# Expert weights: pair 3 of the first expert stage, and quarters 2 and 3 of odd pairs, in pieces of 2 MB

## The chip, the cores and the metric

The kernel runs on one core of a Trainium2 chip. The metric is the device time of one execution in microseconds (us), as the median of repeated runs. The inputs and weights lie in the chip's memory (HBM), all in 32-bit floats, and the kernel has to read them itself.

## The reference, cut to what matters

The program is a small network of four layers over 256 tokens of width 1024. Two layers mix retention and block attention. A third layer (RWKV-like mixing) and a fourth (differential attention and a state space model, "s5") are each followed by a mixture of experts. The change touches only the two mixtures of experts:

```
def hier_moe(h, w_group, b_group, w_expert, b_expert, w_gate, w_up, w_down):
    ...
    top_p, top_j = lax.top_k(e_prob, MOE_TOP_K)
    gates = g_w[:, None] * top_p / jnp.sum(top_p, axis=-1, keepdims=True)
    ...
    y = routed_experts(hf, expert_idx, gates, w_gate, w_up, w_down)

    def run_block(args):
        tok, e, gt = args
        xb = h_pad[tok]
        hidden = jax.nn.silu(xb @ w_gate[e]) * (xb @ w_up[e])
        return (hidden @ w_down[e]) * gt[:, None].astype(xb.dtype)
```

There are 32 experts in each stage, with w_gate and w_up of 1024x512 and w_down of 512x1024. Each token goes to two of them, so nearly every expert has work and the kernel reads all of them: 32 x 3 x 512 x 1024 x 4 bytes = 201 MB a stage.

## The kernel before, in words

An expert stage (`expert_functions`) works on 16 **pairs** of experts, numbered 0 to 15. The weights of a pair are 12 MB, laid out as six **pieces** of 2 MB (128 partitions x 16 KB). Pieces 0 to 3 are the **quarters** of gate and up (a quarter is 256 of the 1024 input features), and pieces 4 and 5 are the **halves** of down. In HBM two neighbouring pieces lie side by side, so pieces 0+1, 2+3 or 4+5 can be had with one transfer of 4 MB with rows of 32 KB (a "wide" load).

TensorE (PE) does for each pair, in this order (`of_pair`): quarters 0 to 3 (L3160, 16 profile records each, results in one PSUM bank), two transposes (L3190), the gathering of the next pair's tokens (L3127), the transposes of the hidden layer (L3197), down half 0 and half 1 (L3174), and the scattering back to the tokens (L3208). `gate_up` and `down` wait with `arrived` for the weights. For a piece that came in a wide load only its even piece has a wait, since both share one semaphore. The last pair of a stage has a form of its own, `of_last`: after each of quarters 0, 1 and 2 it issues six filler matmuls (`keep_clock`, L2814, 12 records), which compute nothing that is used. Further fillers stand later in it.

SyncE (SP) issues all weight loads from one queue, strictly in the order of the code (`sync`). In front of each load stands `released`, a wait until PE has used up what lies in the destination. With several pieces in one load, SP waits for the last of them. Bank 0 means even pairs, bank 1 odd pairs.

- Stage 0 (layer 3 of 4, semaphores moe0) has one set of six slots, the ring, from pair 3 on. Pair 0 is in the ring before the stage starts and pair 1 in spare memory elsewhere (`second`). Pair 2 goes to ring slots 1 to 5 and a spare slot (`third`). Half 1 of pair 1 takes part of ring slot 0. Then comes pair 3, which is written out by hand (L2954 to L2963): pieces 0+1 wide, three small transfers with s5 parameters (512 KB each), pieces 2+3 wide, piece 4, piece 5. Pairs 4 to 15 are loaded by `load_later` in a loop.
- Stage 1 (layer 4, moe1) has two sets of slots, so its loads run two pairs ahead. `load_later` serves it from pair 3 on.
- `alone` lists for each bank the pieces that `load_later` loads one by one. Before: none in even pairs, 4 and 5 in odd pairs.

After stage 0 the same queue sends the next layer's weights into the ring (L262).

Of the kernel before, what the change touches and what calls it, by code (L numbers as in the profile page):

```python
# [40 lines left out]
SLOTS = 6  # L41
# [2810 lines left out]
class Experts:  # L2852


    def __init__(self, g, ly, c0, router):
        self.sync, self.scalar, self.vector, self.tensor, self.gpsimd = expert_functions(g, ly, c0, router)


def expert_functions(g, ly, c0, router):
# [3 lines left out]
    nc, A, ps = g.nc, g.A, g.ps  # L2863
# [8 lines left out]
    landed = g.moe_landed[ly]  # L2872
    first = [[w] for w in ring]
    if ly == 0:
        second = [[g.spare], extra[0], extra[1], extra[2], extra[3], [g.xs_flat, ring[0][:, 0:2048]]]
        third = first[1:] + [[g.spare]]
        later = [first, first]
        later_wide = [moe_ring_wide(g, c0), moe_ring_wide(g, c0)]
        lag = 1
    else:  # L2880
# [3 lines left out]
        later = [first, second]  # L2884
        later_wide = [moe_ring_wide(g, c0), wide]
        lag = 2
    pieces = lambda where: [len(parts) for parts in where]
    early = [[a + b for a, b in zip(pieces(first), pieces(third))],
             pieces(second) if ly == 0 else [1, 1, 2, 1, 1, 2]]
    alone = ((), (4, 5))  # L2890

    def up_w(where, j, e):

# [17 lines left out]
    def turns(eng):  # L2911
        eng.wait_ge(router.s_turns, 1)
        return eng.value_load(g.turns[0:1, 0:1], min_val=1, max_val=S // CAP)
# [11 lines left out]
    def sync(sp):  # L2925
        def released(j, n, more):
            sp.wait_ge(*((s_gu, n * 4 + (more * 4 + j - 3)) if j < 4 else ((s_da, s_dn)[j - 4], n + more)))


        def load(where, bank, pair, j):  # L2930

            sp.dma_start(where[j][0], moe_piece(A, ly, pair, j)).then_inc(landed[bank][j], 16)

        def load_later(bank, pair, n, more):

            for d in range(SLOTS // 2):
                if 2 * d in alone[bank]:
                    for j in (2 * d, 2 * d + 1):
                        released(j, n, more)
                        load(later[bank], bank, pair, j)  # L2940
                else:
                    released(2 * d + 1, n, more)
                    sp.dma_start(later_wide[bank][d], A["moe_weights"][ly, pair, d]).then_inc(landed[bank][2 * d], 16)

        if ly == 0:
            released(0, 0, 1)
            router.part_of(sp, 5, 1, second[5][1])
            for j in range(SLOTS):
                if j < 5:
                    released(j + 1, 0, 1)  # L2950
                else:
                    released(0, 0, 2)
                load(third, 0, 2, j)
            released(5, 0, 2)  # L2954
            for d in range(2):
                released(2 * d, 0, 3)
                sp.dma_start(later_wide[1][d], A["moe_weights"][ly, 3, d]).then_inc(landed[1][2 * d], 16)
                if d == 0:
                    for dst, name in ((g.s5.B[:, 0], "s5_b"), (g.s5.C[0], "s5_c"), (g.s5.bT, "s5_bT")):
                        sp.dma_start(dst, A[name]).then_inc(g.s5_bc_landed, 16)  # L2960
            for j in alone[1]:
                released(j - 1, 0, 3)
                load(later[1], 1, 3, j)  # L2963
        else:
            for j in range(SLOTS):
                released(j, 0, 1)
                load(third, 0, 2, j)
            load_later(1, 3, 0, 2)
        T = turns(sp)
        with sp.Fori(0, T) as t:  # L2970
            with sp.Fori(0, NP // 2 - 2) as i:
                for bank in range(2):
                    load_later(bank, i * 2 + (4 + bank), t * NP + i * 2, 5 + bank - lag)
            with sp.If(t < T - 1):
                for pair in range(4):
                    load_later(pair % 2, pair, t * NP, NP + pair + 1 - lag)
        g.limit = len(g.chunks)
        g.free_when = {}
        if c0 < g.limit:
            for j in range(SLOTS):  # L2980
                sp.wait_ge(*((s_gu, T * NP * 4) if j < 4 else ((s_da, s_dn)[j - 4], T * NP)))
                g.send(sp, c0 + j + 1)
        else:
            for j in range(4):
                at = (slice(None), j // 2, slice((j % 2) * 512, (j % 2 + 1) * 512))
                sp.wait_ge(s_add, j + 1)
                sp.dma_start(g.out[0].rearrange("(a p) n -> p a n", p=P)[at], g.x[at]).then_inc(g.out_written, 16)
            sp.wait_ge(g.out_written, 64)
# [133 lines left out]
    def tensor(pe):  # L3122
# [19 lines left out]
        def arrived(bank, j, rounds):  # L3142

            if j % 2 == 0 or j in alone[bank]:
                pe.wait_ge(landed[bank][j], rounds * 16 + 16 * early[bank][j])

        def arrived_early(pair, j):

# [2 lines left out]
        def gate_up(quarter, where, bank, rounds):  # L3151
            if rounds is None:
                arrived_early(bank, quarter)
            else:
                arrived(bank, quarter, rounds)
            for k in range(2):
                for which in range(2):
                    for e in range(2):
                        q = (2 * which + e) * CAP
                        ins = pe.matmul(b_gu[q:q + CAP, :], xg[:, 2 * quarter + k, e * CAP:(e + 1) * CAP],  # L3160
                                        up_w(where, quarter, e)[:, which, k, :], start=(quarter == 0 and k == 0),
                                        stop=(quarter == 3 and k == 1), tile_position=(0, q))
            ins.then_inc(s_gu, 1)

        def down(half, where, bank, rounds):
            if rounds is None:
                arrived_early(bank, 4 + half)
            else:
                arrived(bank, 4 + half, rounds)
            for f in range(2):  # L3170
                for nh in range(2):
                    for e in range(2):
                        q = (2 * nh + e) * CAP
                        ins = pe.matmul(b_dn[q:q + CAP, :], hidT[:, 2 * half + f, e * CAP:(e + 1) * CAP],  # L3174
                                        down_w(where, 4 + half, e)[:, f, nh * 512:(nh + 1) * 512],
                                        start=(half == 0 and f == 0), stop=(half == 1 and f == 1), tile_position=(0, q))
            return ins
# [75 lines left out]
        if ly == 0:  # L3253
# [10 lines left out]
            router.keep_clock(pe, 5)  # L3264

    return sync, scalar, vector, tensor, gpsimd if ly == 0 else None


# [10 lines left out]
def moe_ring_wide(g, c0):  # L3279

    firsts = MOE_SLOTS[::2] if c0 == N_LOW else range(0, SLOTS, 2)
    return [g.ring[:, at:at + 2, :].rearrange("p s n -> p (s n)") for at in firsts]


def moe_piece(A, ly, pair, j):

    return A["moe_weights"][ly, pair, j // 2][:, (j % 2) * SW:(j % 2 + 1) * SW]
# [104 lines left out]
```

## Time and profile before

| | |
|---|---|
| median of 3 runs | 1549.54 us (1548.98 to 1549.82) |
| the profiled execution's own time | 1549.55 us |
| its span in the trace | 1547.4 us |
| PE busy | 1302.0 us (84%) |
| DVE, ACT, POOL busy | 458.6, 278.1, 265.8 us |
| read from HBM | 495.11 MB, 321 GB/s over the span |
| stage 0, about | 540 to 980 us of the span |
| stage 1, about | 1119 to 1543 us of the span |

The page cuts the span into 40 slices of 38.7 us. For each slice it gives the busy tenths of the engines, the clock that TensorE was granted (PEclk, 9 is 90% or more of full speed), and the busy share and rate of the 16 DMA engines. A busy DMA share of 9 at about 430 GB/s, slice after slice, marks the two expert stages. Between them lies the fourth layer's mixing part, where the DMA engines are partly idle. "Idle before" in a row of the timeline is the time in which the engine did nothing before that instruction, with the one that ended it.

### The profile page before, as it was taken

The page shows a single profiled execution, that of the slowest core. Times are in us where ns is not written, and L with a number is a line of the kernel's source. Part 1 is how long each engine was busy: PE and PEld are TensorE (multiplying, and loading weights), DVE is VectorE, ACT ScalarE, POOL GpSimd, SP SyncE. Part 2 cuts the span into 40 slices and gives each one's busy share as a digit, 9 for nine tenths or more (in the row PEclk, how much of TensorE's full clock was granted, in tenths as well). Part 3 has the DMA queues.
Part 4 walks back from the last instruction along what each step waited for, and adds up shares of the span by engine and source line. Part 5 has one row for each costly group of instructions (what it writes and reads, how often), then busy time and mean ns, then how long its engine had stood idle before and what let it go on. Part 6 is the DMA issues. An engine that isn't in the chain of part 4 may idle for free.

```text
span 1547.4 us, 22048 instructions
## 1 busy us (share of the span) xinstructions
PE 1302.0 (84%) x9344; PEld 711.9 (46%) x9344; DVE 458.6 (30%) x904; ACT 278.1 (18%) x545; POOL 265.8 (17%) x158
## 2 busy tenths in 40 slices
PE   9999999999999997766766767999999676677676
PEld 5754466547878543322322323656544232232233
DVE  2454663654945520200100100276411010010011
ACT  2142410433321210210000000215211011011010
POOL 0675236640000008591000000000000000000000
PEclk9999999999999999888888998999999888888889
DMA  9922562336431798999999999945799999999997
GB/s 372 364 114 82 200 228 71 154 142 274 162 125 42 289 393 357 438 425 431 434 434 426 435 427 431 377 157 208 287 423 429 427 437 429 429 434 430 430 437 296
DMA packets 34355, 498.19 MB, mean 322 GB/s; under 512 B 5488, under 2 KB 8304, under 8 KB 12016
## 3 DMA queue, kind: packets, MB, share of 16 engines
q1 hardware_dynamic: 34288, 497.22, 77.2%
q8 instruction: 52, 0.85, 0.2%
q14 instruction: 15, 0.12, 0.0%
HBM read 495.11 MB, written 2.10 MB: 321 GB/s over the span
## 4 chain that ended last, share of the span: by engine, by line
PE 43%; DMA 23%; another core or an unknown queue 5%; DVE 3%; ACT 1%; issue 1%; SPq 0%; DVEq 0%; ACTq 0%
DMA weight_ring<-in_moe_weights 19%; PE banks L3160 14%; PE banks L3174 5%; PE banks L3127 3%; PE banks L338 3%; DMA x_normed_hT_mix<-in_moe_weights 3%; PE banks L3208 2%; PE banks L1777 2%; PE banks L1970 2%; PE banks L2573 2%; PE banks L2482 1%; PE banks L2814 1%; PE banks L1318 1%; PE banks L1902 1%
## 5 line engine op out<-in xcount | busy, mean ns | idle before, releaser
L3160 PE MATMUL banks<-weight_ring,spare_weights_arena 128*32 128x512 f32 x1472 | 211.3, 724 | 143.1 <-DMA weight_ring<-in_moe_weights 141.5
L3070 DVE TENSOR_TENSOR spare_weights_arena<-spare_weights_arena,banks 64x512 f32<-64x512 f32 x32 | 22.1, 690 | 671.7 <-ACT spare_weights_arena L2993 671.7
L3160 PEld LDWEIGHTS banks<-weight_ring,spare_weights_arena 128*32 128x32 f32 x1472 | 56.0, 129 | 287.7 <-issue 268.5
L2993 ACT ACTIVATE spare_weights_arena<-banks 64x512 f32<-64x512 f32 x32 | 18.9, 592 | 509.8 <-PE banks L3160 509.8
L3127 PE MATMUL banks<-spare_weights_arena,x 128*128 128x64 f32 x960 | 110.5, 273 | 0.0
L3127 PEld LDWEIGHTS banks<-spare_weights_arena,x 128*128 128x128 f32 x960 | 109.6, 192 | 0.0
L3174 PE MATMUL banks<-weight_ring,spare_weights_arena 128*32 128x512 f32 x728 | 95.0, 661 | 12.0 <-issue 6.1
L986 POOL TENSOR_TENSOR weight_ring<-spare_weights_arena,weight_ring 128x2048 f32<-128x2048 f32 x16 | 74.0, 4632 | 70.4 <-DVE spare_weights_arena L830 38.5
L1099 PE MATMUL banks<-weight_ring,x_normed_hT_mix 128*128 128x512 f32 x192 | 84.8, 593 | 0.0
L3208 PE MATMUL banks<-spare_weights_arena 64*128 64x512 f32 x240 | 59.6, 615 | 21.0 <-ACT spare_weights_arena L2999 21.0
L3160 PE MATMUL banks<-x_normed_hT_mix,spare_weights_arena 128*32 128x512 f32 x272 | 42.2, 773 | 31.6 <-DMA x_normed_hT_mix<-in_moe_weights 31.6
L338 PE MATMUL banks<-weight_ring,x_normed_hT_mix 128*128 128x512 f32 x128 | 56.3, 595 | 0.0
L1067 PE MATMUL banks<-x_normed_hT_mix,weight_ring 128*128 128x256 f32 x256 | 56.0, 379 | 0.0
L3174 PEld LDWEIGHTS banks<-weight_ring,spare_weights_arena 128*32 128x32 f32 x728 | 26.9, 119 | 61.1 <-issue 51.2
L1099 PEld LDWEIGHTS banks<-weight_ring,x_normed_hT_mix 128*128 128x128 f32 x192 | 35.7, 190 | 41.5 <-issue 41.4
L986 POOL TENSOR_TENSOR weight_ring<-weight_ring 128x512 f32<-128x512 f32 (+1 forms) x14 | 37.9, 2724 | 81.6 <-DMA weight_ring<-in_ring_weights 74.5
L1067 PEld LDWEIGHTS banks<-x_normed_hT_mix,weight_ring 128*128 128x128 f32 x256 | 48.4, 190 | 7.6 <-issue 1.2
L3208 PEld LDWEIGHTS banks<-spare_weights_arena 64*128 64x128 f32 x240 | 20.7, 186 | 62.3 <-ACT spare_weights_arena L2999 48.2
L3051 DVE TENSOR_TENSOR spare_weights_arena<-banks,spare_weights_arena 128x256 f32<-128x256 f32 x64 | 27.0, 425 | 62.1 <-PE banks L3127 62.0
L3160 PE MATMUL banks<-spare_weights_arena 128*32 128x512 f32 x304 | 35.6, 607 | 11.7 <-DMA spare_weights_arena<-in_moe_weights 11.7
L2999 ACT COPY spare_weights_arena<-banks 128x512 f32<-128x512 f32 x32 | 18.8, 587 | 139.5 <-PE banks L3174 139.5
L1073 PE MATMUL banks<-weight_ring,x_normed_hT_mix 128*128 128x512 f32 x96 | 41.8, 593 | 0.2 <-DVE x_normed_hT_mix L415 0.2
(547 smaller groups left out, 1841.5 us busy)
## 6 DMA issues: line engine op xcount, KB each, us to landing
weight_ring<-in_moe_weights SPq DMA_DIRECT2D x50, 4096.0 KB, 25.2
weight_ring<-in_moe_weights SPq DMA_DIRECT2D x37, 2048.0 KB, 13.7
weight_ring<-in_ring_weights SPq DMA_DIRECT2D x35, 2048.0 KB, 12.1
spare_weights_arena<-in_moe_weights SPq DMA_DIRECT2D x21, 2048.0 KB, 49.6
spare_weights_arena<-in_moe_weights SPq DMA_DIRECT2D x7, 4096.0 KB, 54.5
x_normed_hT_mix<-in_moe_weights SPq DMA_DIRECT2D x7, 4096.0 KB, 51.8
weight_ring<-in_ring_weights SPq DMA_DIRECT2D x4, 1024.0 KB, 5.9
x_normed_hT_mix<-in_moe_weights SPq DMA_DIRECT2D x4, 1024.0 KB, 4.8
```

The costliest lines, as they stand in the source:

```text
L338: ins = pe.matmul(bank, lhsT[:, k, tt * P:(tt + 1) * P], w[:, k, n], start=(k == 0), stop=(k == k_all - 1))
L986: sub = lambda out, left, right: pool.tensor_tensor(out, left, right, ALU.subtract)
L1067: ins = pe.matmul(bank[:, hh * S:(hh + 1) * S], w[:, k, h * P:(h + 1) * P], g.hT[:, k, :], start=(k == 0), stop=(k == KT - 1))
L1073: ins = pe.matmul(bank, g.hT[:, k, half * P:(half + 1) * P], w[:, k, :], start=(k == 0), stop=(k == KT - 1))
L1099: ins = pe.matmul(at_ps[n - 1], left[:, k, :], right[:, k, :], start=(n != P2 and k == 0), stop=(k == HT - 1), skip_group_check=n in (P1, P2))
L1777: ins = pe.matmul(bank[:, i * S:(i + 1) * S], w[:, kt, n:n + P], g.hT[:, kt, :], start=(kt == 0), stop=(kt == KT - 1))
L1970: ins = pe.matmul(ps[j], g.mixT[:, kt, tt * P:(tt + 1) * P], w[:, kt, :], start=(kt == 4), stop=(kt == 3))
L2573: ins = pe.matmul(ps[j], g.mixT[:, k, tt * P:(tt + 1) * P], w[:, k, :], start=(k == 4), stop=(k == 3))
L3127: ins = pe.matmul((b_x, b_dn)[k // 4][:, k % 4 * 2 * CAP:(k % 4 + 1) * 2 * CAP], g.x[:, tt, k * P:(k + 1) * P], Pr[:, tt, :], start=(tt == ...
L3160: ins = pe.matmul(b_gu[q:q + CAP, :], xg[:, 2 * quarter + k, e * CAP:(e + 1) * CAP], up_w(where, quarter, e)[:, which, k, :], start=(quart ...
L3174: ins = pe.matmul(b_dn[q:q + CAP, :], hidT[:, 2 * half + f, e * CAP:(e + 1) * CAP], down_w(where, 4 + half, e)[:, f, nh * 512:(nh + 1) * 512],
L3208: pe.matmul(ps[2 * tt + nh][:, :], PT[r, tt * P:(tt + 1) * P], y[r, :], start=opens, stop=True, skip_group_check=True).then_inc(s_sum[2 * ...
```

## The change

In both stages pieces 2 and 3 of odd pairs are now loaded one by one (`alone`), as 4 and 5 already were. In stage 0, pair 3 is loaded in six single pieces, and each load has its own `released` wait. Piece 0 waits only for half 1 of pair 1, whose data lay in ring slot 0. Piece j after that waits for piece j-1 of pair 2, whose data lay in ring slot j. Before, the wide load 0+1 waited for both conditions of its two pieces, and so did 2+3 with theirs. On PE, quarter 3 of odd pairs gets a wait of its own. The count that the wait for quarters 0 and 1 compares with goes up by one load in stage 0, since pair 3 now brings those two quarters as two loads.

```
-    alone = ((), (4, 5))
+    pair_3_apart = 1 if ly == 0 else 0
+    alone = ((), (2, 3, 4, 5))
...
-            released(5, 0, 2)
-            for d in range(2):
-                released(2 * d, 0, 3)
-                sp.dma_start(later_wide[1][d], A["moe_weights"][ly, 3, d]).then_inc(landed[1][2 * d], 16)
-                if d == 0:
+            for j in range(SLOTS):
+                if j == 0:
+                    released(5, 0, 2)
+                else:
+                    released(j - 1, 0, 3)
+                if j == 1:
+                    sp.dma_start(later[1][1][0], moe_piece(A, ly, 3, 1)).then_inc(landed[1][0], 16)
+                else:
+                    load(later[1], 1, 3, j)
+                if j == 0:
                     for dst, name in ((g.s5.B[:, 0], "s5_b"), (g.s5.C[0], "s5_c"), (g.s5.bT, "s5_bT")):
                         sp.dma_start(dst, A[name]).then_inc(g.s5_bc_landed, 16)
-            for j in alone[1]:
-                released(j - 1, 0, 3)
-                load(later[1], 1, 3, j)
...
             if j % 2 == 0 or j in alone[bank]:
-                pe.wait_ge(landed[bank][j], rounds * 16 + 16 * early[bank][j])
+                pe.wait_ge(landed[bank][j], rounds * 16 + 16 * (early[bank][j] + (pair_3_apart if (bank, j) == (1, 0) else 0)))
```

SP's queue at pair 3 of stage 0. `first_e_normed` is the semaphore here that counts quarters done (`s_gu`), and `moe0_down` counts pairs whose half 1 is done. Before:

```order
L2932 DMA spare_weights_arena<-in_moe_weights 128x4096 [waits first_e_normed]
L2957 DMA weight_ring<-in_moe_weights 128x8192 [waits first_e_normed,moe0_down]
L2960 DMA spare_weights_arena<-in_s_b 128x1024
L2960 DMA spare_weights_arena<-in_s_c 128x1024
L2960 DMA spare_weights_arena<-in_s_bT 128x1024
L2957 DMA weight_ring<-in_moe_weights 128x8192 [waits first_e_normed]
L2932 DMA weight_ring<-in_moe_weights 128x4096 [waits first_e_normed]
L2932 DMA weight_ring<-in_moe_weights 128x4096 [waits moe0_down_half]
```

And now:

```order
L2933 DMA spare_weights_arena<-in_moe_weights 128x4096 [waits first_e_normed]
L2933 DMA weight_ring<-in_moe_weights 128x4096 [waits moe0_down]
L2966 DMA spare_weights_arena<-in_s_b 128x1024
L2966 DMA spare_weights_arena<-in_s_c 128x1024
L2966 DMA spare_weights_arena<-in_s_bT 128x1024
L2961 DMA weight_ring<-in_moe_weights 128x4096 [waits first_e_normed]
L2933 DMA weight_ring<-in_moe_weights 128x4096 [waits first_e_normed] x3
L2933 DMA weight_ring<-in_moe_weights 128x4096 [waits moe0_down_half]
```

The first load of pair 3 and the three s5 transfers behind it no longer wait for a quarter of pair 2. The wait for that quarter now stands in front of piece 1.

PE's queue in the last pair of stage 0, quarters 2 and 3 with the filler matmuls between them. Before:

```order
L3160 MATMUL banks<-weight_ring,spare_weights_arena 32x512 [waits moe0_odd_pairs_landed_2,first_e_root]
L3160 MATMUL banks<-weight_ring,spare_weights_arena 32x512 x7
L2814 MATMUL banks<-resident_constants 128x128 x6
L3160 MATMUL banks<-weight_ring,spare_weights_arena 32x512 x8
L3220 MATMUL banks<-resident_constants,spare_weights_arena 128x128 [waits first_mixT]
```

And now:

```order
L3163 MATMUL banks<-weight_ring,spare_weights_arena 32x512 [waits moe0_odd_pairs_landed_2]
L3163 MATMUL banks<-weight_ring,spare_weights_arena 32x512 x7
L2814 MATMUL banks<-resident_constants 128x128 x6
L3163 MATMUL banks<-weight_ring,spare_weights_arena 32x512 [waits moe0_odd_pairs_landed_3]
L3163 MATMUL banks<-weight_ring,spare_weights_arena 32x512 x7
L3223 MATMUL banks<-resident_constants,spare_weights_arena 128x128 [waits first_mixT]
```

Quarter 3 has a landing to wait for, and quarter 2 now waits for 2 MB where it waited for 4.

## Rows read from the trace of the kernel before

**Rows 1.** The page: section 2, slices of 38.7 us, and section 4, the chain by line.

```profile
DMA  9922562336431798999999999945799999999997
...
DMA weight_ring<-in_moe_weights 19%; PE banks L3160 14%; PE banks L3174 5%; PE banks L3127 3%; PE banks L338 3%; DMA x_normed_hT_mix<-in_moe_weights 3%; PE banks L3208 2%; PE banks L1777 2%; PE banks L1970 2%; PE banks L2573 2%; PE banks L2482 1%; PE banks L2814 1%; PE banks L1318 1%; PE banks L1902 1%
```

**Rows 2.** Windows: stretch, its length, busy us by engine, clock, DMA share, GB/s.

```profile
580.00:586.00 6.00, 5.30 (x41) 1.62 (x40) 0.00 (x0) 0.59 (x1) 3.85 (x14) 1.00 0.00 0
612.00:962.00 350.00, 245.07 (x1740) 106.86 (x1740) 35.16 (x85) 31.75 (x63) 67.36 (x66) 0.87 1.00 431
```

**Rows 3.** Timeline of SP's loads, 578 to 606 us: start, duration, line, operation.

```profile
585.10 0.34 SPq L2957 DMA_DIRECT2D weight_ring<-in_moe_weights  x1
...
590.18 7.19 SPq L2932 DMA_DIRECT2D weight_ring<-in_moe_weights  x2
```

**Rows 4.** Timeline of PE, 578 to 613 us; idle before in brackets.

```profile
579.84 0.59 PE L3174 MATMUL banks<-weight_ring,spare_weights_arena 128*32 128x512 f32 x1
...
583.05 7.07 PE L3160 MATMUL banks<-weight_ring,spare_weights_arena 128*32 128x512 f32 x64
...
601.32 3.64 PE L3160 MATMUL banks<-weight_ring,spare_weights_arena 128*32 128x512 f32 x32
612.28 5.56 PE L3160 MATMUL banks<-weight_ring,spare_weights_arena 128*32 128x512 f32 x32 [7.32 <-DMA weight_ring<-in_moe_weights]
```

**Rows 5.** The chain in order of time, stage 0: start, duration, what.

```profile
641.48 6.36 PE banks L3160 x32
...
670.62 5.44 PE banks L3160 x32
...
699.85 6.19 PE banks L3160 x32
```

**Rows 6.** Line 2932, all its loads: shortest, median, longest time to landing.

```profile
DMA to landing us min/median/max: 7.5/23.8/54.4
```

**Rows 7.** Line 2932, window 948.5 to 950: half 1 of stage 0's last pair.

```profile
L2932 SPq DMA_DIRECT2D weight_ring<-in_moe_weights x1: 332/332/332, 949.3 to 949.3; - x1
...
DMA to landing us min/median/max: 22.9/22.9/22.9
```

**Rows 8.** Line 2932, window 940 to 948.5: half 0 of the same pair.

```profile
L2932 SPq DMA_DIRECT2D weight_ring<-in_moe_weights x1: 333/333/333, 947.5 to 947.5; - x1
...
DMA to landing us min/median/max: 19.8/19.8/19.8
```

**Rows 9.** Timeline of PE, end of stage 0.

```profile
957.93 1.60 PE L2814 MATMUL banks<-resident_constants 128*128 128x128 f32 x12
962.49 1.92 PE L3160 MATMUL banks<-weight_ring,spare_weights_arena 128*32 128x512 f32 x16 [2.96 <-DMA weight_ring<-in_moe_weights]
...
965.88 1.92 PE L3160 MATMUL banks<-weight_ring,spare_weights_arena 128*32 128x512 f32 x16
...
972.45 4.68 PE L3174 MATMUL banks<-weight_ring,spare_weights_arena 128*32 128x512 f32 x32
```

**Rows 10.** Timeline of PE, end of stage 1.

```profile
1523.27 1.60 PE L2814 MATMUL banks<-resident_constants 128*128 128x128 f32 x12
1526.14 1.92 PE L3160 MATMUL banks<-x_normed_hT_mix,spare_weights_arena 128*32 128x512 f32 x16 [1.26 <-DMA x_normed_hT_mix<-in_moe_weights]
...
1529.53 1.92 PE L3160 MATMUL banks<-x_normed_hT_mix,spare_weights_arena 128*32 128x512 f32 x16
...
1535.52 3.64 PE L3174 MATMUL banks<-spare_weights_arena 128*32 128x512 f32 x32
```

**Rows 11.** Line 2932, window 1482 to 1484: half 1 of stage 1's last pair.

```profile
L2932 SPq DMA_DIRECT2D spare_weights_arena<-in_moe_weights x1: 333/333/333, 1482.7 to 1482.7; - x1
...
DMA to landing us min/median/max: 53.1/53.1/53.1
```

**Rows 12.** Timeline of PE after stage 0: the next layer's first projection.

```profile
984.62 3.83 PE L2482 MATMUL banks<-x_normed_hT_mix,weight_ring 128*128 128x128 f32 x32
```

**Rows 13.** Line 262, window 967 to 968: the load that this projection reads.

```profile
DMA to landing us min/median/max: 9.2/9.2/9.2
```

## The prediction, made before the result

> **What bounds the kernel now.** I read the page first. Its slices show the DMA engines at 9 tenths through both expert stages, and by line the largest share of the chain that ended last is a weight load, 19% plus 3% for the one into x_normed_hT_mix [rows 1]. The windows say how full that is: from 612 to 962 us the DMA share is 1.00 at 431 GB/s, while PE is busy 245 of 350 us [rows 2]. So within a stage only two things move its end: the time the DMA engines need for the bytes, and any time in which their queue is empty. What PE does in between counts only if it releases a slot too late, or after the last landings. Three places were left to look at: where the stage begins, what a piece costs, and what follows the last landings.
>
> The beginning has a hole. From 580 to 586 us the DMA share is 0.00 and 0 GB/s, with PE busy 5.30 of 6 us [rows 2]. SP's timeline says why: the next load, pieces 0+1 of pair 3, goes out at 585.10 [rows 3]. That is when PE has finished quarter 0 of pair 2, a quarter of the 7.07 us that began at 583.05. Its other condition, half 1 of pair 1, had ended at 579.84 + 0.59 = 580.43 [rows 4]. PE pays for the hole at 612.28, after 7.32 us of waiting for pieces 2+3 of pair 3 [rows 4]. From there the stage runs in step with the landings.
>
> At the end of each stage PE stands still until pieces 2+3 of the last pair are there (2.96 us in stage 0, 1.26 us in stage 1), and only then does quarter 2, then fillers, then quarter 3 [rows 9, 10].
>
> **The hole (gain 4.6 us).** Piece 0 of pair 3 now waits for 580.43 alone. SP issues 0.06 us after PE's last instruction of that kind (quarter 3 ends at 583.05 + 7.07 = 590.12, the load stands at 590.18 [rows 3, 4]), so at 580.5 instead of 585.1: 4.6 us. For this to count, the queue must not run empty again behind it. It then holds 2 MB and the three s5 transfers, 3.5 MB or 8.5 us at 431 GB/s, which lasts to about 589. Piece 1 goes out at 585.1, when quarter 0 of pair 2 is done, pieces 2, 3 and 4 by 590.18, when its last quarter is, and piece 5 at 597, the second of the two loads that began at 590.18 [rows 3]. Every one is in the queue before the one ahead of it is through. PE reaches pair 3 at 601.32 as before [rows 4], since it is busy with pair 2 until then. Its quarters 0 and 1 landed long before. Pieces 2+3 land at 612.28 - 4.6 = 607.7, later than PE's 601.32 + 3.64 = 605.0, so the whole 4.6 us reaches PE. At each later step the landings lead, and the shift stays. Bounds: no more than the hole itself, whose end is fixed by 585.10 - 580.43 = 4.7 us. If pair 3 were not limited by its landings it would be 0. I take 4.6, because PE's wait of 7.32 us exceeds it.
>
> **The price of a single piece (loss 1.1 us).** A 4 MB load becomes two of 2 MB in pair 3 of stage 0 twice, in its pairs 5, 7, ... 15 once (6), and in pairs 3, 5, ... 15 of stage 1 once (7), 15 in all. The trace has the same comparison already: the step from one landing of 2+3 to the next holds 4+5 once wide (even pairs) and once single (odd pairs). Wide: 670.62 - 641.48 = 29.14. Single: 699.85 - 670.62 = 29.23 [rows 5]. That is 0.09 us a split here; the nine further steps of the stage repeat the pattern between 29.14 and 29.23, and I take 0.07. 15 x 0.07 = 1.1 us (0.6 in stage 0, 0.5 in stage 1), all of it on the path, since the DMA engines are the path. Bounds: 0 at one end. At the other end stands a load into an empty queue, which took 7.5 us to land [rows 6], where inside a full queue two such landings lie 949.3 + 22.9 - (947.5 + 19.8) = 4.9 us apart [rows 7, 8]. That would be 2.6 us a split. The rows of the full queue are the same case as ours, so I stay at 0.07. The instructions added on SP (fourteen in its program, some 0.3 us per load) lie beside its waits.
>
> The Trainium skill, "DMA: Bandwidth & Descriptors", section on the anatomy of one DMA, fits a transfer as about 2.0 us fixed plus bytes / 436 GB/s. Read as a cost for each transfer in turn, it would speak against this change: 15 more transfers would be 30 us. The spacing of 4.9 us for 2 MB above is the bytes alone at 431 GB/s, so the trace agrees only with the second term while the queue is full. The fixed part shows up only when the queue was empty.
>
> **The end of stage 0 (gain 3.0 us).** Piece 2 of the last pair now lands one piece, 4.9 us, ahead of piece 3, at 962.4 - 4.9 = 957.5 on the old time scale. PE is then still in the fillers behind quarter 1, which begin at 957.93 and take 1.5 (as after quarter 2: from 962.49 + 1.9 to 965.88). So quarter 2 runs from 959.5 to 961.3, its fillers to 962.9, and quarter 3, landed at 962.4, begins at 962.9 instead of 965.88 [rows 9]. What follows hangs on quarter 3 only: silu, transposes, hidden layer, down at 972.45 - 3.0 = 969.5, where half 0 has landed (947.5 + 19.8 = 967.3 [rows 8]). Half 1 lands at 949.3 + 22.9 = 972.2 [rows 7] and takes 1.8 us of PE (3.64 / 2 at full clock [rows 10]), so down can't end before 974.0. Before, it ended at 977.1, and 3.0 less is 974.1. The two limits meet. The gain is 3.0, at most 3.1. PE's clock sets the lower bound: down took 4.68 us here, against 3.64 in the same work at full clock [rows 9, 10]. If the half level (1.2 GHz instead of 2.4) falls on both quarters and the fillers between, 1.6 us of it go, and 1.4 is left. The next layer takes the shift over. Its first projection starts at 984.62 [rows 12], and its weights, issued when quarter 3 is done at 965.88 + 1.92 = 967.8, landed 9.2 us later, at 977.0 [rows 9, 13]. Those move by only 4.6 - 0.6 = 4.0, PE by 7.0, and of the 7.6 us between them 4.6 remain.
>
> **The end of stage 1 (gain 1.35 us).** The same steps: the fillers behind quarter 1 begin at 1523.27 and end at 1524.8, quarter 2 runs to 1526.65, its fillers to 1528.2, against 1529.53 before for quarter 3 [rows 10]. Piece 3 landed at 1526.1, so nothing but PE's own queue is in the way. Down starts at 1534.2 and half 1 of it at 1536.0, just after its landing at 1482.7 + 53.1 = 1535.8 [rows 11]. The bounds are 0 and 1.5. There is no hole at the start of this stage that the change could close: its pieces 0+1 and all of pairs 0 to 2 are loaded as before.
>
> **PE's new wait.** In odd pairs quarter 3 waits for its own landing. Queued behind it are the transposes, the gathering for the next pair and down, which need or follow quarter 3 anyway, and the landing comes when 2+3 came. Quarter 2 is done earlier, which only releases a slot earlier. In the full queue that is worth nothing.
>
> **Sum.** 4.6 + 3.0 + 1.35 - 1.1 = 7.85 us. The profiled execution took 1549.55 us (span 1547.4), practically the median of the runs, 1549.54. That gives 1549.55 - 7.85 = 1541.7 us.
>
> **Rivals.** (a) The ends give nothing: PE falls to the lower clock now that it has no pause before quarter 2, or something else than quarter 3 holds down back. For it: the granted clock was only 0.87 over the stage [rows 2]. Against: the fillers already kept PE going through both ends before. Time: 1549.55 - 4.6 + 1.1 = 1546.05. (b) The hole moves instead of closing: pair 3 starts early, but PE, which is busy from 583 to 605 without a gap, becomes what the next landings wait for. For it: in that stretch PE has hardly a gap, 5.30 busy of 6 us in the hole itself [rows 2]. Against: the wait of 7.32 us [rows 4], and later on loads of 4.9 us each land 19.8 and 22.9 us after their issue [rows 7, 8], so that some 15 us of queue cover a late release. Time: 1549.55 - 4.35 + 1.1 = 1546.3. (c) Slower: a split costs as much as a load on its own. Its place is each of the 15 split loads, its price 2.6 us [rows 6 to 8], and it decides from 8.95 / 15 = 0.6 us a split on. At the full price the time is 1549.55 - 8.95 + 39 = 1579.6. Against it stands the 29.23 beside 29.14 [rows 5]. The rule of the Trainium skill above would put it at 1549.55 - 8.95 + 30 = 1570.6.
>
> **Chances and range.** Forecast 0.81, (a) 0.07, (b) 0.05, (c) 0.03, and 0.04 for something that eats all of it and leaves no change. Two runs of this kernel can be told apart from about 0.2%, 3.1 us, on. (a) and (b) just clear that and count as faster: 0.93. Same 0.04, slower 0.03. The forecast's own range is 1540.0 (every gain at its upper bound, splits for nothing: 4.7 + 3.1 + 1.5 = 9.3) to 1544.5 (both ends at their lower bounds, 1.4 + 0). With (a) and (b) it reaches to 1546.3.
>
> **What would show it.** In the new profile the DMA share of the window from 580 to 586 us is well over a half instead of 0.00, and SP's first load of pair 3 stands at 580.5. PE's first wait for pieces of pair 3 ends near 607.7, now in front of quarter 3. The step between landings of 2+3 has one more 0.07 us. At the end of stage 0 quarters 2 and 3 follow each other with only fillers between, and down ends 3.0 us nearer to the landing of 0+1 than before. In stage 1 that is 1.35 less the split's share. The forecast is wrong if PE waits for DMA between 605 and 641 as late as before, if the DMA share falls below 1.00 somewhere in pairs 3 to 15, or if down in the last pair waits for half 1 by more than a few tenths.

## The result, and the profile after

| | before | changed |
|---|---|---|
| median, four runs each | 1549.68 us | 1540.11 us (1539.12 to 1541.48) |
| profiled execution, its span | 1549.55, 1547.4 us | 1540.02, 1537.0 us |

The ratio is 0.9935 with a 95% interval of 0.9918 to 0.9953. On the first median of before that is 1539.5 us, or 10.1 us faster. I had forecast 7.85 us (a ratio of 0.9949), with 1540.0 us as the lower end of the range. The direction and the order of size were right, but the gain came out larger than the range allows by that ratio. With all runs, those made later too (68 of before, 16 of the change), the means are 1549.5 and 1541.0: 8.5 us, give or take 1.0. One slow execution of before (1865.85 us, granted clock 0.674 over its span) is left out of every number here. So most of the surplus belongs to the spread of the first eight runs, and a smaller part to a term that I sized too small.

The page of the changed kernel, the slices of the DMA engines (section 2):

```profile
DMA  9922452336430699999999999945799999999997
```

The stages are as full as before [rows 1]. What changed is the places where they begin and end. First the hole. SP's timeline of the changed kernel around pair 3 of stage 0:

```profile
576.96 0.33 SPq L2933 DMA_DIRECT2D weight_ring<-in_moe_weights  x1
577.33 0.43 SPq L2966 DMA_DIRECT2D spare_weights_arena<-in_s_b  x1
...
581.50 0.33 SPq L2961 DMA_DIRECT2D weight_ring<-in_moe_weights  x1
583.22 10.62 SPq L2933 DMA_DIRECT2D weight_ring<-in_moe_weights  x4
```

The windows there (stretch, length, busy us by engine, granted clock, DMA share, GB/s):

```profile
541.00:577.00 36.00, 34.19 (x294) 17.06 (x286) 8.80 (x34) 6.46 (x13) 0.00 (x0) 1.00 1.00 417
578.00:582.00 4.00, 4.00 (x32) 1.19 (x32) 0.00 (x0) 0.00 (x0) 3.02 (x13) 1.00 0.98 377
580.00:586.00 6.00, 6.00 (x64) 1.79 (x56) 0.00 (x0) 0.00 (x0) 5.26 (x9) 1.00 0.98 410
```

And PE, with the wait that had been 7.32 us at 612.28 [rows 4]:

```profile
579.52 7.07 PE L3163 MATMUL banks<-weight_ring,spare_weights_arena 128*32 128x512 f32 x64
...
597.79 5.36 PE L3163 MATMUL banks<-weight_ring,spare_weights_arena 128*32 128x512 f32 x48
604.13 1.92 PE L3163 MATMUL banks<-weight_ring,spare_weights_arena 128*32 128x512 f32 x16 [0.97 <-DMA weight_ring<-in_moe_weights]
```

The load of piece 0 stands 4.54 us ahead of that of piece 1, which still waits for quarter 0 of pair 2. That is the hole's 4.6 us. PE runs quarters 0 to 2 of pair 3 in one go and waits 0.97 us for quarter 3. But the whole picture stands earlier than that explains: quarter 0 of pair 2 starts at 579.52 instead of 583.05 [rows 4], before any changed load could matter. The window from 541 to 577 says why: a granted clock of 1.00. In the first profile of before, two stretches in the same work were at half:

```profile
541.10:544.50 3.40, 3.40 (x18) 0.79 (x10) 0.00 (x0) 0.00 (x0) 0.00 (x0) 0.50 1.00 417
575.20:578.60 3.40, 3.40 (x20) 1.11 (x23) 0.45 (x2) 0.00 (x0) 0.00 (x0) 0.51 0.88 376
```

So the window from 580 to 586 us, which I had named as a sign, doesn't test the change: it covers other work in the new profile than in the old one. A second profile of before, made later, has a full-clock opening too, and its pair 0 starts at 540.56 us where that of the change starts at 540.62. Its windows, with no edit at all:

```profile
578.00:582.00 4.00, 4.00 (x32) 1.20 (x32) 0.00 (x0) 0.00 (x0) 3.00 (x14) 1.00 0.07 29
580.00:586.00 6.00, 6.00 (x64) 1.73 (x56) 0.00 (x0) 0.00 (x0) 5.33 (x9) 1.00 0.70 251
```

The fair pair of windows is 578 to 582 us: 0.07 before, 0.98 with the change. There the hole is closed.

The ends, as PE's timeline shows them. Stage 0 of the changed kernel:

```profile
945.02 1.92 PE L3163 MATMUL banks<-weight_ring,spare_weights_arena 128*32 128x512 f32 x16 [2.46 <-DMA weight_ring<-in_moe_weights]
...
950.27 1.60 PE L2814 MATMUL banks<-resident_constants 128*128 128x128 f32 x12
951.80 1.92 PE L3163 MATMUL banks<-weight_ring,spare_weights_arena 128*32 128x512 f32 x16
...
955.19 1.92 PE L3163 MATMUL banks<-weight_ring,spare_weights_arena 128*32 128x512 f32 x16
...
961.82 4.70 PE L3177 MATMUL banks<-weight_ring,spare_weights_arena 128*32 128x512 f32 x32
```

And stage 1:

```profile
1507.24 1.92 PE L3163 MATMUL banks<-spare_weights_arena 128*32 128x512 f32 x16 [1.97 <-DMA spare_weights_arena<-in_moe_weights]
...
1517.41 1.92 PE L3163 MATMUL banks<-x_normed_hT_mix,spare_weights_arena 128*32 128x512 f32 x16
...
1523.40 1.92 PE L3177 MATMUL banks<-spare_weights_arena 128*32 128x512 f32 x16
1526.81 1.92 PE L3177 MATMUL banks<-spare_weights_arena 128*32 128x512 f32 x16 [1.49 <-DMA spare_weights_arena<-in_moe_weights]
```

Quarter 2 follows quarter 1 with only the fillers between, where PE had stood for 2.96 and 1.26 us [rows 9, 10]. What ends last now is half 1 of down: it waits 1.49 us for its landing in stage 1. In stage 0 down ran partly at the half clock (4.70 us), which took up that wait; in the second profile of the change it ran at full clock there, and half 1 waited 1.50 us. I had named such a wait, "by more than a few tenths", as a sign that the forecast is wrong, and it came. For stage 1 I had placed the start of down by an execution in which quarter 0 and the fillers behind it were partly at half clock.

### The profile page after: what moved, and what is told of

Same layout as the page of the kernel before. It is cut to its first block, busy times and chain, and to the rows that moved or that the text cites. A ratio compares the mean times of both kernels' runs of the same rounds, so it can differ in the third digit from the quotient of the medians.

```text
span 1537.0 us, 22091 instructions
## 1 busy us (share of the span) xinstructions
PE 1307.8 (85%) x9344; PEld 713.2 (46%) x9344; DVE 460.4 (30%) x904; ACT 278.2 (18%) x545; POOL 265.9 (17%) x158
## 4 chain that ended last, share of the span: by engine, by line
PE 43%; DMA 22%; another core or an unknown queue 5%; DVE 3%; ACT 1%; issue 1%; SPq 0%; DVEq 0%; ACTq 0%
DMA weight_ring<-in_moe_weights 19%; PE banks L3163 13%; PE banks L3177 5%; PE banks L3130 4%; PE banks L338 3%; DMA x_normed_hT_mix<-in_moe_weights 3%; PE banks L3211 2%; PE banks L1777 2%; PE banks L1970 2%; PE banks L2573 2%; PE banks L2814 1%; PE banks L2482 1%; PE banks L1318 1%; ACT spare_weights_arena L3002 1%
## 5 line engine op out<-in xcount | busy, mean ns | idle before, releaser
L3163 PE MATMUL banks<-weight_ring,spare_weights_arena 128*32 128x512 f32 x1472 | 224.9, 763 | 134.4 <-DMA weight_ring<-in_moe_weights 132.9
L3130 PE MATMUL banks<-spare_weights_arena,x 128*128 128x64 f32 x960 | 115.2, 280 | 0.0
L3130 PEld LDWEIGHTS banks<-spare_weights_arena,x 128*128 128x128 f32 x960 | 114.7, 199 | 0.0
L3177 PE MATMUL banks<-weight_ring,spare_weights_arena 128*32 128x512 f32 x728 | 90.6, 632 | 14.3 <-issue 8.6
L3163 PE MATMUL banks<-x_normed_hT_mix,spare_weights_arena 128*32 128x512 f32 x272 | 35.8, 652 | 19.6 <-DMA x_normed_hT_mix<-in_moe_weights 19.6
```

The source lines that it names most:

```text
L3130: ins = pe.matmul((b_x, b_dn)[k // 4][:, k % 4 * 2 * CAP:(k % 4 + 1) * 2 * CAP], g.x[:, tt, k * P:(k + 1) * P], Pr[:, tt, :], start=(tt == ...
```

## The experiments

To compare profiles in which the clock fell in different places, I cut PE's timeline at the same instructions in each. **Opening** is from the start of pair 0 in stage 0 to the end of down in pair 1, the same work in every kernel, all of it ahead of the hole's end. **Body 0** goes from there to the start of pair 15 (the first instruction of its quarter 0). **End 0** is from there to the end of down in pair 15. **Body 1** is from the start of pair 0 to that of pair 15 in stage 1, and **end 1** as end 0. The mixing part between the stages took 142.4 us in ten profiles and 144.3 in two.

| profile | opening | body 0 | end 0 | body 1 | end 1 |
|---|---|---|---|---|---|
| before | 39.62 | 372.26 | 24.45 | 396.85 | 22.75 |
| before, second | 36.28 | 372.20 | 24.43 | 397.48 | 24.37 |
| only piece 0 early | 36.28 | 367.67 | 22.81 | 396.63 | 24.39 |
| only odd pairs split | 40.39 | 372.76 | 21.62 | 397.12 | 21.46 |
| change | 36.28 | 368.12 | 21.49 | 398.35 | 21.49 |
| change, second | 36.28 | 368.73 | 21.50 | 396.87 | 21.48 |
| change, third | 37.98 | 368.28 | 21.50 | 397.12 | 21.47 |
| split in pair 15 only | 39.61 | 367.85 | 21.38 | 398.11 | 21.46 |
| the same, second | 36.28 | 367.87 | 21.49 | 396.71 | 21.47 |
| all single | 37.54 | 365.15 | 26.30 | 394.41 | 26.20 |
| no fillers | 36.28 | 368.19 | 21.49 | 396.67 | 21.49 |
| fewest pieces | 36.28 | 367.51 | 21.51 | 395.86 | 21.49 |

(With all pieces single, pair 15 starts one piece of 4.8 us earlier, so bodies are shorter and ends longer by that.)

**The hole alone.** From the kernel before:

```
             released(5, 0, 2)
+            sp.dma_start(later[1][0][0], moe_piece(A, ly, 3, 0)).then_inc(landed[1][0], 16)
             for d in range(2):
...
+                if d == 1:
+                    released(0, 0, 3)
+                    sp.dma_start(later[1][1][0], moe_piece(A, ly, 3, 1)).then_inc(landed[1][0], 16)
+                    released(2, 0, 3)
+                    sp.dma_start(later_wide[1][1], A["moe_weights"][ly, 3, 1]).then_inc(landed[1][2], 16)
```

> The kernel before with one edit: pair 3 of stage 0 gets pieces 0 and 1 as single loads, piece 0 behind half 1 of pair 1 alone. Pieces 2+3 stay wide everywhere. My theory (hole closed by what the release of piece 0 gives, 4.6 us, less one split of 0.07): 4.5 us faster than before, ratio 0.9971, and both ends of the stages as long as before (24.5 us from the landing of pieces 0+1 of the last pair to the end of down in stage 0). Rival 1, the whole surplus over my forecast sits in the hole: 7 us faster, 0.9955. Rival 2, the hole is covered anyway and all gain is from the ends: no change, 1.000.

Median 1544.42 us over 12 runs, ratio 0.9968 (0.9954 to 0.9981), 5.0 us. Body 0 is 372.23 (the mean of the two profiles of before) - 367.67 = 4.56 us shorter, the forecast term. Its opening is at full clock as well, so its windows compare with those of the second profile of before (0.14 in the first of them there, 0.70 in the second):

```profile
578.00:580.00 2.00, 2.00 (x16) 0.64 (x16) 0.00 (x0) 0.00 (x0) 1.50 (x7) 1.00 0.91 352
580.00:586.00 6.00, 6.00 (x60) 1.69 (x52) 0.00 (x0) 0.00 (x0) 5.34 (x9) 1.00 0.97 406
```

Rival 2 (no gain from the hole) falls. Rival 1 is not supported: 7 us (0.9955) lies inside the interval by a hair, but body 0 shows no more than 4.56. What I expected of the ends was not so. This kernel has pieces 2+3 wide, and its end 1 took 24.39 us, not the 22.75 that I had read. PE's timeline there:

```profile
1515.92 3.49 PE L3165 MATMUL banks<-x_normed_hT_mix,spare_weights_arena 128*32 128x512 f32 x16 [2.87 <-DMA x_normed_hT_mix<-in_moe_weights]
1519.34 1.69 PE L2814 MATMUL banks<-resident_constants 128*128 128x128 f32 x12
1520.96 1.92 PE L3165 MATMUL banks<-x_normed_hT_mix,spare_weights_arena 128*32 128x512 f32 x16
...
1526.95 3.64 PE L3179 MATMUL banks<-spare_weights_arena 128*32 128x512 f32 x32
```

Quarter 2, after a pause of 2.87 us, took 3.49 us instead of 1.92, at the half level. End 0, on the other hand, was 22.81 us here and not 24.45: no stretch of it was at half clock, and down took 3.64 us instead of 4.68.

The first profile of before had a stretch at half clock in end 1 too, but it lay elsewhere, over quarter 0 and the fillers behind it, ahead of the landing that PE had to wait for:

```profile
1516.41 2.80 PE L3160 MATMUL banks<-spare_weights_arena 128*32 128x512 f32 x16 [2.87 <-DMA spare_weights_arena<-in_moe_weights]
1519.14 2.35 PE L2814 MATMUL banks<-resident_constants 128*128 128x128 f32 x12
```

There it only shortened the pause before quarter 2, to 1.26 us [rows 10]. From the start of the pair to the start of quarter 2 it was 9.7 us in both kernels. So the 1.26 us that I had taken for the size of the wait was what the half clock had left of 2.9.

**The split loads alone.** From the changed kernel, pieces 0+1 of pair 3 wide again:

```
-    pair_3_apart = 1 if ly == 0 else 0
+    pair_3_apart = 0
...
+            released(5, 0, 2)
+            for j in (0, 2, 3, 4, 5):
+                released(max(j - 1, 0), 0, 3)
                 if j == 0:
...
+                    sp.dma_start(later_wide[1][0], A["moe_weights"][ly, 3, 0]).then_inc(landed[1][0], 16)
```

> The changed kernel with pieces 0+1 of pair 3 of stage 0 wide again and behind both of its conditions, as before; pieces 2 and 3 of all odd pairs single. My theory: the hole stays, both ends gain 3.0 and 1.35, 14 splits cost 0.07 each (1.0): 3.35 us faster than before, 0.9978. Rival 1, the stage 1 splits cost 0.25 each as the profile after suggests (1.5 us between stage start and last pair): 2.0 us faster, 0.9987. Rival 2, the surplus over my forecast comes from the split loads in the stages: 5.5 us faster, 0.9965.

Median 1544.26 us over 12 runs, ratio 0.9974 (0.9963 to 0.9986), 4.0 us, where I expected 3.35. Body 0 stays at 372.8, both ends are short. Rival 1 (0.9987) lies just outside the interval. Rival 2 (0.9965, 5.5 us) isn't ruled out by the times, but body 0 and body 1, at 372.76 and 397.12, have nothing that a surplus could sit in. Its opening took 40.39 us, in a span of 1546.5, and the window tells what a single profile can hold:

```profile
534.00:551.10 17.10, 17.10 (x80) 11.42 (x80) 6.28 (x34) 1.59 (x3) 0.00 (x0) 0.50 0.81 332
```

A stretch of 17.1 us at half clock, from ahead of the first pair (its start is at 542.56) to well into it. The two parts together give 5.0 + 4.0 = 9.0 us.

**Split only where an end uses it.** From the changed kernel: pieces 2+3 single in pair 15 alone (and in pair 3 of stage 0). The last pair's loads are taken out of the loop, and PE waits for piece 3 with a constant:

```
-    alone = ((), (2, 3, 4, 5))
+    alone = ((), (4, 5))
...
-            with sp.Fori(0, NP // 2 - 2) as i:
+            with sp.Fori(0, NP // 2 - 3) as i:
...
+            with sp.If(t > T - 2):
+                load_later(1, NP - 1, t * NP + (NP - 6), 6 - lag, (2, 3, 4, 5))
```

> The changed kernel with pieces 2+3 single only where an end uses them, in pair 15 of each stage, and pair 3 of stage 0 in six pieces as in the change. Pieces 2+3 of pairs 5 to 13 of stage 0 and 3 to 13 of stage 1 are wide again: 11 splits fewer. At 0.07 us each: 0.8 us faster than the change, 1539.3 us where that has 1540.1. If a split costs 0.25 us in stage 1: 0.35 + 1.5 = 1.9 us faster, 1538.2. If early release of single pieces is worth something within a stage (rival): slower than the change by 1 us or more.

Median 1538.47 us over 5 runs, ratio 0.9931 (0.9915 to 0.9947). Its profile happens to have the same half-clock stretches in the opening as the first one of before (39.61 and 39.62 us), so the two compare directly. Piece 0 of pair 3 is issued at 580.42 where the wide load had been at 585.10, as forecast. The queue had run empty by then (its DMA share from 579 to 580 us is 0.08), so a slow opening leaves some of the hole open even with the change, and the gain is what the earlier issue gives: pair 15 starts 407.46 us after pair 0 where it was 411.88, 4.42 us less, against 4.6 - 0.15 from my terms. The rival (early release is worth something within a stage) falls: body 0 isn't longer than in the change, 367.85 against 368.12. Its body 1, with no split in it, took 398.11. So the 398.35 of the first profile of the change was no price of splits, and my reading of 0.25 us a split was wrong.

**Everything single.** From the changed kernel. Piece 1 of pair 3 counts on a semaphore of its own here like all others:

```
-    pair_3_apart = 1 if ly == 0 else 0
-    alone = ((), (2, 3, 4, 5))
+    pair_3_apart = 0
+    alone = (tuple(range(6)), tuple(range(6)))
```

> The changed kernel with every load of load_later single, each with its own wait on PE: 49 splits more than the change (24 in stage 0, 25 in stage 1). It measures the price of a split by itself. At 0.07 us: 3.4 us slower than the change, 1543.5. At 0.25 us: 12 us slower, 1552. At 2.6 us, the latency of a lone load: 127 us slower. If a split costs nothing: 1540, since the ends are already bound by the landing of half 1.

Median 1544.5 us over 12 runs, ratio 0.9970 (0.9956 to 0.9984): slower than the change by 3.5 to 4.4 us, expected 3.4. Pair 15 begins at its piece 0 and not at piece 1, 4.83 us earlier (26.30 less the usual 21.47), so body 0 compares as 365.15 + 4.83 = 369.98. Against 367.86 with the split in pair 15 only, that is 2.12 us for 29 splits (the 24 of stage 0 and the 5 that this kernel has beyond pair 15's), 0.073 each. In stage 1 the same way gives 394.41 + 4.72 (26.20 less 21.48) = 399.13 against 397.2 without the splits, 2.0 us for 31 of them or 0.06 each, with single profiles 1.7 us apart. The rival of 2.6 us a split is out by a factor of 30. So is the reading of the Trainium skill ("DMA: Bandwidth & Descriptors", anatomy of one DMA) that gives each transfer in turn 2.0 us of its own; that page of the skill gives the fit for transfers on GpSimd's path, and the loads here are issued by SP.

The 2.6 us rested on a misread row. The load that landed after 7.5 us [rows 6] is the one issued at 547.33, and the queue wasn't empty: the load of 1 MB issued at 544.25 landed 5.7 us later, at 549.95, and this one 4.9 us behind it, the spacing of a full queue. No run here times a load of 2 MB by itself.

**The change again.** No edit.

> The changed kernel, unedited. In single profiles the opening of stage 0 (start of pair 0 to the end of down in pair 1, the same instructions in every kernel) took 36.3 to 40.4 us, by how much of it was granted the half clock, and single runs of the kernel before span 10 us. My theory: the surplus of the first comparison (ratio 0.9935, where I forecast 0.9949) is this spread; more runs give 7.9 us, 0.9949 or between that and 0.994. Rival: the change itself does 10 us: 0.9935 again, with an opening of 36.3 us in this profile again and no half clock before 620 us.

Median 1540.55 us over 6 runs, ratio 0.9941 (0.9922 to 0.9960): 9.1 us, at the upper edge of what I allowed for. The rival's 0.9935 is inside the interval, so the times alone don't refute it. The profile has a full-clock opening again, as the rival wanted, but also a stretch at half clock before 620 us (590.98 to 594.39).

**Before again.** No edit.

> The kernel before, unedited, for a second look at its opening. My theory: the half clock falls elsewhere than in the first profile (then 541.1 and 575.2 us), the opening takes anything from 36.3 to 40.4 us, and the landing of pair 15's pieces 0+1 in stage 0 follows with 372.3 us from the end of the opening (411.88 - 39.62), within 0.3. Rival: the windows belong to the program and stand where they stood.

Ratio 0.9996 (0.9977 to 1.0015) over 8 runs. The opening took 36.28 us, full clock, and body 0 372.20, for which I had forecast 372.3. So the half-clock stretches of the opening don't belong to the program. What surprised was end 1:

```profile
1523.07 3.18 PE L3160 MATMUL banks<-x_normed_hT_mix,spare_weights_arena 128*32 128x512 f32 x16 [2.86 <-DMA x_normed_hT_mix<-in_moe_weights]
1526.18 1.99 PE L2814 MATMUL banks<-resident_constants 128*128 128x128 f32 x12
1528.10 1.92 PE L3160 MATMUL banks<-x_normed_hT_mix,spare_weights_arena 128*32 128x512 f32 x16
```

Here too quarter 2 after the pause ran partly at the lower level (3.18 us), and the end took 24.37 us, not 22.75 [rows 10].

**Split in pair 15 only, again.** No edit.

> The kernel with pieces 2+3 single only in pair 15 of each stage, unedited from the first time (then five runs, ratio 0.9931). My theory: 11 splits fewer than the change are worth 0.8 us: ratio 0.9944 when the change has 0.9949. Rival: no difference to the change, since a split costs nothing. With single runs 2 to 3 us apart I expect the two only just to be told apart, if at all.

Median 1537.67 us over 6 runs, ratio 0.9925 (0.9904 to 0.9946). Over both sets the mean of 11 runs is 1538.9 us, 2.1 less than the change's 1541.0 over 16. The splits that it saves account for 0.8. The intervals of the two ratios overlap, and I don't claim more than the 0.8.

**No fillers behind quarters 0 to 2 of the last pair.** From the changed kernel:

```
-                if quarter < 3:
-                    router.keep_clock(pe, 6)
```

> The changed kernel without the filler matmuls behind quarters 0, 1 and 2 of the last pair. My theory: with piece 2 landing by itself these fillers hold up only quarter 3, by 0.4 us in each stage, and half 1 of down lands too late for PE to use that: no change to the changed kernel, at most 0.3 us a stage faster, quarter 3 starting within 0.1 us of its landing. Rival: without them PE falls to the half clock for what follows quarter 3, and each end gets 1.6 us or more longer than the 21.5 us of the change.

Median 1540.46 us over 6 runs, ratio 0.9940 (0.9920 to 0.9961), like the change (0.9941 on the same chip). End 0 in its profile:

```profile
950.12 1.92 PE L3163 MATMUL banks<-weight_ring,spare_weights_arena 128*32 128x512 f32 x16 [1.26 <-DMA weight_ring<-in_moe_weights]
955.00 1.92 PE L3163 MATMUL banks<-weight_ring,spare_weights_arena 128*32 128x512 f32 x16 [2.96 <-DMA weight_ring<-in_moe_weights]
...
960.99 1.92 PE L3177 MATMUL banks<-weight_ring,spare_weights_arena 128*32 128x512 f32 x16
964.79 1.92 PE L3177 MATMUL banks<-weight_ring,spare_weights_arena 128*32 128x512 f32 x16 [1.88 <-DMA weight_ring<-in_moe_weights]
```

Quarters 2 and 3 now wait for their landings, quarter 3 starts 9.78 us after the pair instead of 10.17, and half 1 of down waits 1.88 us. The end stays 21.49. The rival (half clock without fillers) didn't come true in this profile: all four rows are 1.92 us, and neither end has a stretch at half clock. One profile can't say that it never does.

**Fewest pieces.** As with the split in pair 15 only, and 4+5 wide too except there:

```
-    alone = ((), (4, 5))
+    alone = ((), ())
```

> As the kernel with pieces 2+3 single only in pair 15, and now pieces 4+5 of odd pairs are wide too except in pair 15 (and in pair 3 of stage 0, which keeps six single pieces): 11 splits fewer again, 22 fewer than the change. My theory: 22 x 0.07 = 1.5 us faster than the change, which has about 1540.7 over its ten runs, so 1539.2; from the end of the opening to pair 15's pieces 0+1 in stage 0 367.5 us (367.9 with 4+5 single), the end of the stage 21.5 us after that as before. Rival: with 4+5 wide the slot of half 0 is released late and the queue runs low: 369 us or more and slower than the change.

Median 1539.21 us over 6 runs, ratio 0.9934 (0.9920 to 0.9949). Body 0 is 367.51 as forecast (367.5), end 0 21.51, and the queue stays full (DMA share 1.00 from 607 to 944 us):

```profile
607.00:944.00 337.00, 234.34 (x1651) 101.81 (x1649) 37.57 (x85) 31.40 (x63) 68.86 (x66) 0.86 1.00 432
```

The rival of a low queue falls. Of the kernels tried, the last two kinds have the lowest times, both below the change by 1.8 to 2.1 us in the mean, at the edge of what these runs can tell.

**The change, third set.** No edit.

> The changed kernel, unedited, for a third set of runs. My theory, with the ends of both stages now sized from all profiles (22.8 or 24.4 us without the split, 21.5 with it): 4.6 + 2.4 + 2.4 - 1.1 = 8.3 us faster than before, ratio 0.9946 give or take 0.001. Rival: 10 us, 0.9935, as in the first comparison.

Median 1540.98 us over 6 runs, ratio 0.9948 (0.9933 to 0.9964), 8.1 us, where the terms sized anew give 8.3. The 10 us of the first comparison (0.9935) stands just inside the lower edge of this interval.

## Why the prediction was right or wrong, point by point

- **The hole, 4.6 us: right.** Body 0 shows 4.56 in the kernel with only that edit, and the load of piece 0 stands 4.54 us ahead of that of piece 1. The sign that I named for it, the window from 580 to 586 us, was a bad one: it fills up to 0.70 in the kernel before as soon as the opening runs at full clock.
- **The price of a split, 0.07 us: right in stage 0.** All single gives 0.073, and the change's body 0 (368.33 in the mean of four profiles with its loads) less 367.86 is 0.47 for 5 splits, 0.09. In stage 1 the six splits of the change don't stand out: 397.2 in the mean of five profiles with them, 397.2 in the mean of five without, single profiles 1.7 us apart. The upper bound of 2.6 us came from a load that was not alone in the queue.
- **The end of stage 0, 3.0 us: right for that profile, and by luck in part.** 24.45 became 21.49, and quarter 3 moved by what I forecast. But 1.6 us of the 24.45 was half clock behind quarter 3, in the last fillers and in down, and where it didn't fall there the unsplit end took 22.81. Without the split it ranges from 22.81 to 24.45, with it the end stays at 21.4 to 21.6. In the mean the gain is 2.4.
- **The end of stage 1, 1.35 us, with 1.5 as its upper bound: too small.** This is the term of the sum that was mis-sized. I read it from an execution in which the half clock fell on quarter 0, where it cost nothing and hid part of the pause, and in which quarter 2 ran at full clock. In the two other profiles of the unsplit end quarter 2 took 3.18 and 3.49 us, and the end 24.4 us. The gain is 2.9 then, 1.3 otherwise, 2.4 in the mean.
- **The direction that I gave PE's clock: wrong.** I used the clock only as something that could take from the gain. In fact an unsplit end grows by 1.6 us when a stretch at half clock falls behind its last wait. A split end, bound by the landing of half 1, has about 1.5 us to spare: in the third profile of the change quarter 3 came 11.8 us after the pair's start instead of 10.2, and the end was 21.50 all the same. Whether the split also makes such stretches rarer stays open.
- **The sum's base: right as a number.** 1549.55 us is also the mean of 68 runs (1549.5). It was luck in its parts: this execution had lost 39.62 - 36.28 = 3.3 us to two half-clock stretches in its opening and had a short end 1. The step between the first two profiles, 9.5 us, is 3.3 from the opening, 4.1 from body 0, 3.0 and 1.3 from the ends, less 1.5 in body 1 and some 0.9 of time outside the span. In that pair the terms themselves are as forecast, and the opening, which no edit touches, makes the surplus.
- **The range: too narrow.** It had no term for the spread. A single run of the kernel before lies anywhere from 1544.1 to 1555.2 (standard deviation 2.5 us). The first four of before were 0.7 us above the mean of all its runs and the first four of the change 0.8 us below. A lower end 1.7 us under the forecast, from bounds of the terms alone, left no room for that. Its sums are also rounded outwards: 1549.55 - 9.3 is 1540.25, not 1540.0, and the upper end comes to 1544.65, not 1544.5.
- **The rivals.** (a) The ends give something (4.0 us by themselves). (b) The hole's 4.6 us reach the end of body 0. (c) is refuted by the single loads.

In sum the terms now are 4.6 + 2.4 + 2.4 - 1.1 = 8.3 us, against 8.5 over all runs. The new sizes were read from profiles of the same kernels, so this agreement shows that no large term is missing, and is not a forecast that came true. The two ends changed by -0.6 and +1.05, so the better sizes add only 0.45 us to the 7.85. The rest of the first comparison's 10.1 us lies within its own interval (0.9918 to 0.9953, or 7.3 to 12.7 us).

## What to carry to other kernels

Where the DMA queue sets the pace, as in these two stages, the size of a piece mattered little (0.07 us for cutting 4 MB in two), and what counted was that the queue doesn't run empty and that little work is left behind the last landing. So cut loads only where a release would otherwise come late or where the last one is waited for, and leave the rest wide. Before sizing a term from one profile, look which granted clock its rows had: slow rows ahead of a wait hide part of it, slow rows behind it add to its end, and a slow stretch in unchanged work is not the change's. Before naming a window as a sign, ask what shifts it besides the change.

## What the runs showed of the hardware that I had not expected

- Stretches at half clock (1.2 instead of 2.4 GHz) in the opening, where PE is busy nearly all the time: none in seven of twelve profiles, two of 3.4 us in two others, one of 3.4 us in another, and in two the end of one that had begun before it (10.2 and 17.1 us long). They move from run to run with the same program, and take up to 4.1 us (36.28 to 40.39).
- After a pause of 2.86 or 2.87 us, quarter 2 took 3.18 and 3.49 us, against 1.92 at full clock. In the profile where it took 1.92 us after 1.26 us of pause [rows 10], quarter 0 had taken 2.80 us after a pause of 2.87. In stage 0 quarter 2 took 1.92 us after 2.96 us of pause [rows 9]. So such a pause is not always followed by the lower clock, and what decides it stays open.
- Two landings of 2 MB in a full queue took 0.07 to 0.09 us more than one of 4 MB, over 29 splits in a stage.
